# Hybrid gMLP and band-attention step: head pairs handled two to a cycle, with whole-row turning runs, streams beside the pairs and y gated in place

## The chip, the cores and the metric

One core of a Trainium2 chip runs the whole program in one launch. The metric is the device time of that launch in microseconds (us); the median of three runs stands for a kernel. Engines are named as in the profile: PE is TensorE, PEld its weight load, DVE VectorE, ACT ScalarE, POOL GpSimd, SP SyncE (here a DMA queue only).

## What is computed

2048 prompt tokens and 8 streams of 16 tokens (17 tiles of 128 tokens, width 1024) go through one layer:

```python
h = einsum(x, w_in)                       # u, v_a, z_a, q, k, v_b, z_b
u, v_a = gelu(h_u), layernorm(gelu(h_va))
a_out = u * (tril(w_s) @ v_a + b_s)       # chunks of 128, 4 groups
p = softmax(q @ k.T / 8 + rel_bias)       # chunk of 64 queries, its own and 8 chunks before, 8 heads
b_out = p @ v_b
y = concat(a_out * silu(z_a), b_out * silu(z_b))
out = layernorm(2**0.25 * x + y @ w_out)
```

The streams do the same with 128 cached keys and 16 new ones. The arithmetic is fp32, and each big product is made of three products of operands that are split into a high and a low part (high by high, high by low, low by high).

## The kernel before, in words

**Projections.** All groups of `w_in` are multiplied first, by `project_chunk` and `project_tile`. The last group, v, goes tile by tile (24 products of 128x512 a tile): the first `V_EARLY` = 9 tiles by themselves, and the other 8 inside the next stage, in halves.

**The paired stage.** A list `UNITS` holds 72 units: for each prompt tile t four "pair" units (two heads each), and after each of the tiles 4 to 11 one "stream" unit. One step of every engine's loop handles one unit, and PE's step is: `scores` of unit s (12 products from tile 4 on, 64 rows by 128 columns, two heads side by side, L1256), `turn(s-1, 0)` (up to 8 blocks of the probabilities transposed, in 16 half transposes, L1290), a `quarter` of dense work (12 products of 128x512: half a v tile up to step 15, L1186, then half of a half of the output projection, L1351), `turn(s-1, 1)` (the fifth key tile: 2 blocks, 4 half transposes, from tile 4 on), and `weigh(s-1)` (the weighted sums, up to 20 products, 128 rows by 64 columns, L1328). The output projection of tile n starts at step 16 + 4n (`START`).

**Around it.** DVE adds the bias and takes the row minimum (`add_bias`, L1050), then `normalise` multiplies by one over the row sum (L1067, L1069). ACT takes the exponent with its sum (L878) and copies the transposes out of PSUM (`copy_turned`, L871, two copies a unit from tile 4 on). After the fourth pair of a tile DVE's `gate` (L1076) multiplies the sums by z into a staging tile, SP stores it to `s_y` (L610), and `load_y` (L550) later brings the whole y tile back. ACT rounds it (`y_high_part`, L895), and DVE subtracts (L1139). After a half of the output projection DVE adds the residual (L1098) and takes statistics (L1101, L1109). POOL makes 1/sqrt(var) (L731, L733) and, for all but the last `TAIL` = 3 tiles, three passes over 128x1024: subtract and scale (L737), times gain (L740), plus offset (L742). For the last tiles DVE does it (`finish`). POOL also splits the output weights in eight parts j (`split_wo`, L716 and L718): parts 0 to 3 are loaded when v tile 13 is projected, and parts 4 to 7 when v tile 16 is. The first half of the output projection needs parts 0 to 3, the second parts 4 to 7.

**Order.** Every queue is written out by hand. All waits are on counting semaphores, and each engine runs its own list in order. SP issues nearly all DMAs and waits in its own list. The order of the tiles is 0 to 14, the streams' tile, then 15 (`ORDER`).

Of the kernel before, what the change touches and what calls it, by code (L numbers as in the profile page):

```python
# [33 lines left out]
TAIL = 3  # L34
# [23 lines left out]
V_EARLY = 9  # L58
# [70 lines left out]
STREAM_AFTER = 4  # L129

# [6 lines left out]
def unit_order():  # L137
    units = []
    for t in range(PTILES):
        units += [("pair", t, p) for p in range(GRP)]  # L140
        if STREAM_AFTER <= t < STREAM_AFTER + SB:
            units.append(("stream", t - STREAM_AFTER, None))
    return units


UNITS = unit_order()
NU = len(UNITS)
PLACE = {(kind, a, b): u for u, (kind, a, b) in enumerate(UNITS)}


def heads_of(u):
    return 2 if UNITS[u][0] == "pair" else 1


def turned_copies(u):

    kind, t, _ = UNITS[u]
    return 1 + (key_tiles(t) > 4) if kind == "pair" else 2
# [9 lines left out]
HEADS_BEFORE = before(heads_of)  # L168
COPIES_BEFORE = before(turned_copies)
STREAMS_BEFORE = before(lambda u: UNITS[u][0] == "stream")  # L170
TILES_BEFORE = before(lambda u: UNITS[u][0] == "pair" and UNITS[u][2] == GRP - 1)


def gate_step(tile):

    return PLACE["pair", tile, GRP - 1] + 2

V_STEPS = 2 * (TILES - V_EARLY)  # L180
STEPS = V_STEPS + 4 * TILES
ORDER = [*range(PTILES - 1), PTILES, PTILES - 1]
START = [V_STEPS + 4 * n for n in range(TILES)]
SPLIT = [s - 1 for s in START]
GATED = [gate_step(t) for t in range(PTILES)] + [PLACE["stream", SB - 1, None] + 3]
Y_LOAD = [max(START[max(n - 2, 0)] + 1 - 7 * (n < 2), GATED[ORDER[n]] + 1) for n in range(TILES)]
X_LOAD = [V_STEPS, V_STEPS] + [START[n - 2] + 7 for n in range(2, TILES)]
POOL_TILES = TILES - TAIL

# [27 lines left out]
def hybrid_stream_step(nc, x, x_t, w_all, w_o, w_sgu, b_sgu, ln_v_g, ln_v_b, rel_rev, ln_g, ln_b,  # L217
# [6 lines left out]
    with ctx:  # L224
# [11 lines left out]
        s_y = dram("s_y", [2 * GRP, P, T])  # L236
# [48 lines left out]
        prob = [at(f"prob{s}", x_at[1] + 12800 + 2560 * s, [WIN]) for s in range(4)]  # L285
        z = [at(f"z{s}", x_at[1] + 23040 + 2048 * s, [GRP, P]) for s in range(2)]
        pt = [at("pt0", x_at[1] + 27136, [10, P]), at("pt1", u_at, [10, P])]
        low, den, rden = (at(name, x_at[1] + 32256 + 64 * j, [4]) for j, name in enumerate(("low", "den", "rden")))
# [112 lines left out]
        so_kept = sem("so_kept")  # L401
        so_back = sem("so_back")
        ys_ready = sem("ys_ready")
        ys_stored = sem("ys_stored")

# [13 lines left out]
        def slot(unit, h):  # L421
            return (HEADS_BEFORE[unit] + h) % 4
# [1006 lines left out]
```

## Time and profile before

| | |
|---|---|
| median of 3 runs | 1085.3 us (1085.28 to 1085.33) |
| the profiled execution, its own time | 1085.31 us |
| its span in the profile | 1083.3 us |
| busy share of PE / DVE / ACT / POOL | 99% / 43% / 31% / 20% |
| the paired stage | 634 us to 1044 us of the span |

A time in a row is counted in us from the start of the span. A matmul's end is modelled, since matmuls overlap in the array, so the spacing of two starts tells more than the length of one. In the timeline a row is a run of like instructions, with the start of the first and the time to the end of the last. In the chain of waits a row is a piece of the work that ended last.

### The profile page before, as it was taken

To read this page: it belongs to the slowest core of one execution; us is meant where nothing else is said; L and a number is where in the kernel's file an instruction comes from. 1 tells how busy PE (TensorE), PEld (TensorE's weight loads), DVE (VectorE), ACT (ScalarE), POOL (GpSimd) and SP (SyncE) were. 2 spreads that over 40 slices of the span, in tenths; PEclk is the share of its full clock that TensorE was granted. 3 is DMA by queue.
4 is the path that set the end of the run, shared out by engine and by line. 5 is a ranking of instruction groups with operands and counts; after the bars stand their busy time and mean duration, and the time that the engine had idled before them with its cause. 6 is when DMAs were issued, how large, how long until landed. Compare 5 with 4: busy or idle time off the path is not lost.

```text
span 1083.3 us, 17667 instructions
## 1 busy us (share of the span) xinstructions
PE 1068.4 (99%) x7338; PEld 912.4 (84%) x7338; DVE 462.7 (43%) x940; ACT 333.6 (31%) x660; POOL 213.7 (20%) x163
## 2 busy tenths in 40 slices
PE   9999999999999999999999999999999999999997
PEld 7988889999999999999999877777777777788875
DVE  6544441212212111121112014577667767777755
ACT  6410101111111111111112134454554555555530
POOL 0111112010110000000000000553444333444331
PEclk9999999999999999999999999999999999999999
DMA  9561114221211333333331444795555445444422
GB/s 340 194 182 49 39 39 129 73 88 60 73 63 54 117 123 123 117 124 112 119 107 65 126 147 145 214 283 162 156 149 167 124 150 149 129 143 141 127 89 78
DMA packets 129967, 137.34 MB, mean 127 GB/s; under 512 B 7496, under 2 KB 103904, under 8 KB 129888
## 3 DMA queue, kind: packets, MB, share of 16 engines
q1 hardware_dynamic: 124992, 121.54, 35.5%
q10 hardware_dynamic: 4896, 14.68, 4.1%
q8 instruction: 58, 0.95, 0.4%
q14 instruction: 21, 0.17, 0.1%
HBM read 86.62 MB, written 52.72 MB: 129 GB/s over the span
## 4 chain that ended last, share of the span: by engine, by line
PE 93%; DVE 2%; POOL 2%; ACT 1%; DMA 1%; issue 1%; POOLq 0%; DVEq 0%; SPq 0%
PE s_ps L1169 35%; PE s_ps L1186 16%; PE out_ps L1351 14%; PE pt_ps L1169 8%; PE o_ps L1328 6%; PE s_ps L1256 5%; PE pt_ps L1290 4%; PE s_ps L1351 2%; DVE prob L1069 1%; POOL wo_l L718 1%; PE o_ps L1198 1%; PE out_ps L1198 1%; ACT prob L878 1%; DMA bias<-s_skew 1%; DMA wo_raw<-w_o 0%
## 5 line engine op out<-in xcount | busy, mean ns | idle before, releaser
L1169 PE MATMUL s_ps<-xh,ring 128*128 128x512 f32 (+1 forms) x1200 | 341.3, 362 | 0.8 <-ACT st L842 0.8
L1169 PEld LDWEIGHTS s_ps<-xh,ring 128*128 128x128 f32 x1200 | 221.3, 188 | 24.5 <-issue 1.2
L1169 PE MATMUL s_ps<-xl,ring 128*128 128x512 f32 (+1 forms) x600 | 217.2, 362 | 0.0
L1186 PE MATMUL s_ps<-ring,xh 128*128 128x512 f32 x544 | 171.0, 395 | 0.0
L871 ACT ACTIVATE pt<-pt_ps 128x1024 f32<-128x1024 f32 (+3 forms) x112 | 78.9, 704 | 158.6 <-PE pt_ps L1290 158.3
L1169 PEld LDWEIGHTS s_ps<-xl,ring 128*128 128x128 f32 x600 | 112.6, 188 | 11.8
L1186 PEld LDWEIGHTS s_ps<-ring,xh 128*128 128x128 f32 x544 | 99.8, 188 | 20.3
L1186 PE MATMUL s_ps<-ring,xl 128*128 128x512 f32 x272 | 106.1, 390 | 0.0
L1050 DVE CUSTOM_DVE_ANT_1 prob<-s_ps,bias 128x640 f32<-128x640 f32 (+1 forms) x112 | 85.5, 801 | 45.3 <-PE s_ps L1256 45.3
L1351 PE MATMUL out_ps<-wo_h,yh 128*128 128x512 f32 x248 | 103.0, 415 | 0.5 <-POOL wo_l L718 0.5
L878 ACT ACTIVATE prob<-prob,low 128x640 f32<-128x640 f32 (+3 forms) x136 | 100.3, 740 | 5.8 <-DVE low L1050 5.4
L1351 PE MATMUL out_ps<-wo_h,yl 128*128 128x512 f32 x248 | 97.0, 391 | 0.0
L1351 PE MATMUL out_ps<-wo_l,yh 128*128 128x512 f32 x248 | 96.8, 391 | 0.0
L1069 DVE TENSOR_SCALAR prob<-prob,rden 128x640 f32<-128x640 f32 (+4 forms) x136 | 94.6, 695 | 4.8
L1169 PE MATMUL pt_ps<-xh,ring 128*128 128x384 f32 x304 | 80.2, 334 | 0.0
L1328 PE MATMUL o_ps<-pt,v 128*64 128x128 f32 x1120 | 75.3, 278 | 0.0
L963 DVE SCALAR_TENSOR_TENSOR st<-s_ps,st 128x512 fp32r<-128x512 f32 (+1 forms) x32 | 20.0, 624 | 119.0 <-ACT st L803 119.0
L1256 PE MATMUL s_ps<-k,q 64*128 64x256 f32 (+3 forms) x696 | 70.4, 331 | 0.1
L1328 PEld LDWEIGHTS o_ps<-pt,v 128*64 128x64 f32 x1120 | 59.9, 137 | 8.9 <-issue 5.6
L1290 PEld LDWEIGHTS pt_ps<-ident,prob 64*128 64x128 f32 x1120 | 46.1, 138 | 24.7 <-issue 14.0
L952 DVE SCALAR_TENSOR_TENSOR st<-st,s_ps 128x512 f32<-128x512 f32 (+1 forms) x32 | 19.5, 618 | 109.8 <-ACT st L789 109.8
L1256 PEld LDWEIGHTS s_ps<-k,q 64*128 64x128 f32 x696 | 52.2, 185 | 13.4 <-issue 11.3
(138 smaller groups left out, 1237.4 us busy)
## 6 DMA issues: line engine op xcount, KB each, us to landing
raw<-w_all ACTq DMA_DIRECT2D x26, 512.0 KB, 3.6
yr<-s_y SPq DMA_DIRECT2D x17, 512.0 KB, 4.8
r<-x SPq DMA_DIRECT2D x17, 512.0 KB, 3.6
q<-s_q SPq DMA_DIRECT2D x16, 512.0 KB, 4.2
k<-s_k SPq DMA_DIRECT2D x16, 512.0 KB, 5.6
y_out<-r SPq DMA_DIRECT2D x15, 512.0 KB, 3.9
s_y<-st SPq DMA_DIRECT2D x24, 256.0 KB, 2.4
x_raw<-x_t SPq DMA_DIRECT2D x12, 384.0 KB, 12.9
```

Source lines behind the costliest of these rows:

```text
L871: nc.scalar.activation(held, pt_both[:, :, 0:m, :], ACT.Copy).then_inc(pt_copied, 1)
L878: nc.scalar.activation(prob[s][:, 0:n], prob[s][:, 0:n], ACT.Exp, bias=low[:, s:s + 1], scale=-1.0, accum_out=den[:, s:s + 1]).then_inc(ex ...
L963: nc.vector.scalar_tensor_tensor(out=st[s_low][:, 0:n].bitcast(f32r), in0=src, scalar=QSCALE if kind == "q" else 1.0, in1=held, op0=ALU.mu ...
L1050: nc.vector.tensor_tensor_reduce(out=out, in0=src, in1=b, scale=1.0, scalar=MASKED, op0=ALU.add, op1=ALU.min, accum_out=low[:, s:s + 1]).t ...
L1069: nc.vector.tensor_scalar(prob[s][:, lo:n], prob[s][:, lo:n], rden[:, s:s + 1], None, ALU.mult).then_inc(normed, 1)
L1169: last = nc.tensor.matmul(bank[b][:, 0:width], w[:, kc, :], xx[:, kc, :], start=kc == 0 and a == 0, stop=kc == KC - 1 and a == 2)
L1186: last = nc.tensor.matmul(out, xx[:, kc, cols], ring[:, 0:GRP, side, kc, :], start=kc == 0 and a == 0, stop=kc == KC - 1 and a == 2)
L1198: last = nc.tensor.matmul(mix_ps[t % 2][:, g * P:(g + 1) * P], st[t % 2][:, g * P:(g + 1) * P], (wt if t < PTILES else wts)[:, g, :], star ...
L1256: last = nc.tensor.matmul(s_ps[h][:, at_c:at_c + count * P], q[t % 2][rows, a * GRP + p, :], k[rows, c * GRP + p, first * P:(first + count ...
L1290: last = nc.tensor.transpose(pt_both[:, half, i, :], prob[slot(unit, h)][rows, lo + b * P:lo + (b + 1) * P], ident[rows, rows])
L1328: last = nc.tensor.matmul(o_ps[64 * h:64 * h + 64, p * P:(p + 1) * P], v[(t + 1 - nk + b) % KR][:, p * P + 64 * h:p * P + 64 * h + 64], pt ...
L1351: last = nc.tensor.matmul(out_bank(half), y[n % 2][:, c, :], w[h][:, c, :], start=c == 0 and a == 0, stop=c == KC - 1 and a == 2)
```

## The change

- The unit list holds the 64 pair units alone. One **cycle** handles two of them, 2c and 2c+1, in 38 cycles. `V_EARLY` is 13, so that four v tiles are left for cycles 0 to 3. The output projection of tile n is in cycles 4+2n and 5+2n, half of its columns each, 24 products in one run.
- PE's cycle is: turn of unit 2c-2, scores of 2c, the dense run (`middle`), a stream's part, turn of 2c-1, scores of 2c+1, and the sums of 2c-2 and 2c-1 one after the other.
- `turn` transposes all ten blocks in one run. The fifth key tile's two blocks go first, into columns 640 to 767 of the two score banks (`fifth_ps`), and so `turn` waits until both heads of the unit after next in the score order have been biased, and `scores` waits for the fifth tile's copies before its run at column 512. ACT copies the fifth tile in two copies and the rest in one.
- Stream b's scores are in cycle 7+2b, its transposes one cycle later, its sums two cycles later, with buffers and semaphores of their own.
- The y tile's attention half is gated straight into the y buffer (`yr`), so that its store to `s_y` is gone and the load is half as large. `yr` and `yl` share their memory. The streams' tile is last.
- The normalisation's first pass moves from POOL (L737) to ACT (`centre`, an Identity with scale and bias, two cycles after `START`), and POOL makes the bias for it (`shift`). `TAIL` is 4.
- DVE's cycle is: gate, bias of 2c, normalise 2c-1, the stream's normalise, normalise 2c, y's low part, residual, stream bias, stream gate, bias of 2c+1, statistics.

```diff
-V_EARLY = 9
+V_EARLY = 13
-TAIL = 3
+TAIL = 4
+UNITS = [(t, p) for t in range(PTILES) for p in range(GRP)]
+V_CYCLES = TILES - V_EARLY
+CYCLES = V_CYCLES + 2 * TILES
+START = [V_CYCLES + 2 * n for n in range(TILES)]
+STORE = [START[n] + (3 if n < TILES - TAIL else 2) for n in range(TILES)]
+STREAM_IN = [V_CYCLES + 3 + 2 * b for b in range(SB)]
...
+        z = [at(f"z{s}", x_at[2] + 16384 + 2048 * s, [GRP, P]) for s in range(2)]
+        yr = [at(f"yr{s}", x_at[3 + s] + 20480, [KC, P]) for s in range(2)]
+        fifth_ps = [s_ps[half][:, 640:768] for half in range(2)]
...
# SyncE
+                if cycle == 1:
                     sp.wait_ge(proj_done, DONE["v", 13])
                     for j in range(4):
                         load_wo(j)
...
+                if cycle == V_CYCLES - 1:
                     sp.wait_ge(proj_done, DONE["v", TILES - 1])
                     for j in range(4, 8):
                         load_wo(j)
                         if j % 2:
                             load_x(j // 2 - 2)
+                    store_v(V_EARLY + cycle)
...
# GpSimd
-                    nc.gpsimd.tensor_scalar(r[n % 2][:], r[n % 2][:], mv[n % 2][:, 0:1], rstd[n % 2][:],
-                                            ALU.subtract, ALU.mult).then_inc(centred, 1)
+                    nc.gpsimd.tensor_scalar(shift[n % 2][:], mv[n % 2][:, 0:1], rstd[n % 2][:], -1.0,
+                                            ALU.mult, ALU.mult).then_inc(shifted, 1)
                     pool.wait_ge(centred, n + 1)
...
# ScalarE
+            def copy_turned(unit):
...
+                if n > 4:
+                    act.wait_ge(turned, TURNED_BEFORE[unit] + 2)
+                    for half in range(2):
+                        held = pt[unit % 2][:, 8:10, HD * half:HD * half + HD]
+                        nc.scalar.activation(held, fifth_ps[half].rearrange("p (g t) -> p g t", g=2), ACT.Copy).then_inc(pt_copied, 1)
+                act.wait_ge(turned, TURNED_BEFORE[unit + 1])
...
+            def centre(n):
+                act.wait_ge(shifted, n + 1)
+                nc.scalar.activation(r[n % 2][:], r[n % 2][:], ACT.Identity, bias=shift[n % 2][:],
+                                     scale=rstd[n % 2][:]).then_inc(centred, 1)
+
+            for cycle in range(CYCLES):
+                copy_turned(2 * cycle - 2)
+                for h in range(2):
+                    exponent(2 * cycle, h)
+                if 1 <= cycle < V_CYCLES:
+                    copy_v(V_EARLY + cycle - 1)
...
+                    if START[n] - 1 == cycle:
+                        y_high_part(n)
...
+                    if START[n] + 2 == cycle:
+                        centre(n)
+                for b in at_cycle(cycle, -1):
+                    place_stream(b)
+                for b in at_cycle(cycle, 2):
+                    keep_sums(b)
+                for b in at_cycle(cycle, 1):
+                    copy_stream(b)
+                copy_turned(2 * cycle - 1)
+                for b in at_cycle(cycle, 0):
+                    stream_exponent(b)
+                for h in range(2):
+                    exponent(2 * cycle + 1, h)
...
# VectorE
+            for cycle in range(CYCLES):
+                if closes_tile(2 * cycle - 3):
+                    gate(UNITS[2 * cycle - 3][0])
+                biases(2 * cycle)
+                for h in range(2):
+                    normalise(2 * cycle - 1, h)
+                for b in at_cycle(cycle, 1):
+                    normalise_stream(b)
+                for h in range(2):
+                    normalise(2 * cycle, h)
...
+                        y_low_part(n)
...
+                    residual(n, h)
+                for b in at_cycle(cycle, 0):
+                    add_stream_bias(b)
+                for b in at_cycle(cycle, 2):
+                    gate_stream(b)
+                biases(2 * cycle + 1)
+                if n >= 0:
+                    statistics(n, h)
...
# TensorE
+            def turn(unit):
...
+                pe.wait_ge(normed, 2 * unit + 2)
+                if has_fifth(unit):
+                    pe.wait_ge(biased, min(2 * (unit + 2), 2 * NU))
...
+            for cycle in range(CYCLES):
+                turn(2 * cycle - 2)
+                scores(2 * cycle)
+                middle(cycle)
+                for b in at_cycle(cycle, 0):
+                    stream_scores(b, cycle)
+                for b in at_cycle(cycle, 2):
+                    weigh_stream(b, cycle)
+                for b in at_cycle(cycle, 1):
+                    turn_stream(b, cycle)
+                turn(2 * cycle - 1)
+                for b in at_cycle(cycle, 2):
+                    turn_back(b)
+                scores(2 * cycle + 1)
+                weigh(2 * cycle - 2)
+                weigh(2 * cycle - 1)
+                if cycle < V_CYCLES - 1:
+                    project_tile("v", V_EARLY + cycle, KC // 2, KC)
```

## Rows read from the trace of the kernel before

**Rows 1.** The page, busy time by engine.
```profile
PE 1068.4 (99%) x7338; PEld 912.4 (84%) x7338; DVE 462.7 (43%) x940; ACT 333.6 (31%) x660; POOL 213.7 (20%) x163
```
**Rows 2.** Busy time by stretch: span, length, each engine's busy, clock, DMA.
```profile
634.00:1044.20 410.20, 406.99 (x4026) 320.38 (x4024) 274.54 (x660) 211.76 (x458) 153.80 (x86) 1.00 0.52 155
...
996.96:1002.99 6.03, 6.03 (x67) 4.92 (x64) 4.95 (x9) 3.03 (x6) 4.58 (x2) 1.00 0.53 149
```
**Rows 3.** Timeline of PE, one unit: start, length, line, tiles, count.
```profile
1002.99 0.66 PE L1290 MATMUL pt_ps<-ident,prob 64*128 64x64 f32 x16
1003.58 0.50 PE L1351 MATMUL out_ps<-wo_h,yh 128*128 128x512 f32 x1
...
1006.52 0.34 PE L1290 MATMUL pt_ps<-ident,prob 64*128 64x64 f32 x4
1006.79 1.31 PE L1328 MATMUL o_ps<-pt,v 128*64 128x128 f32 x20
1008.03 1.15 PE L1256 MATMUL s_ps<-k,q 64*128 64x256 f32 x12
1009.02 0.66 PE L1290 MATMUL pt_ps<-ident,prob 64*128 64x64 f32 x16
```
**Rows 4.** The chain of waits, one half of the output projection alone.
```profile
1053.86 5.44 PE out_ps L1351 x24
```
**Rows 5.** Timeline of PE, a unit of tile 0: the short runs.
```profile
650.44 0.28 PE L1290 MATMUL pt_ps<-ident,prob 64*128 64x64 f32 x4
650.65 0.73 PE L1186 MATMUL s_ps<-ring,xh 128*128 128x512 f32 x2
...
653.59 0.44 PE L1328 MATMUL o_ps<-pt,v 128*64 128x128 f32 x4
653.96 0.39 PE L1256 MATMUL s_ps<-k,q 64*128 64x256 f32 x2
```
**Rows 6.** Timeline of PE, two waits, with the idle time before the row in brackets.
```profile
638.48 0.34 PE L1290 MATMUL pt_ps<-ident,prob 64*128 64x64 f32 x4 [0.68 <-DVE prob L1069]
...
1048.11 0.50 PE L1351 MATMUL s_ps<-wo_h,yh 128*128 128x512 f32 x1 [0.85 <-DVE r L1098]
```
**Rows 7.** The chain of waits, output weights 4 to 7: load, last split.
```profile
709.31 4.79 DMA wo_raw<-w_o
...
726.34 2.50 POOL wo_l L718
```
**Rows 8.** Groups by form, ACT from 634 us: busy, mean ns; idle before.
```profile
L895 ACT ACTIVATE yh<-yr 128x1024 fp32r<-128x1024 f32 x17 | 17.9, 1051 | 9.5 <-PE s_ps L1351 9.4
...
L901 ACT ACTIVATE so<-o_ps 128x128 f32<-128x128 f32 x8 | 2.2, 278 | 7.2 <-PE o_ps L1316 7.2
```
**Rows 9.** Timeline of ACT, the two exponents of a unit.
```profile
904.34 0.82 ACT L878 ACTIVATE prob<-prob,low 128x640 f32<-128x640 f32 x1
...
905.15 0.82 ACT L878 ACTIVATE prob<-prob,low 128x640 f32<-128x640 f32 x1
```
**Rows 10.** Timeline of DVE, the two biases of a unit.
```profile
1028.03 0.81 DVE L1050 CUSTOM_DVE_ANT_1 prob<-s_ps,bias 128x640 f32<-128x640 f32 x1
...
1028.76 0.82 DVE L1050 CUSTOM_DVE_ANT_1 prob<-s_ps,bias 128x640 f32<-128x640 f32 x1
```
**Rows 11.** Timeline of DVE: normalise beside a POOL pass, without one, of a stream.
```profile
742.17 2.65 DVE L1069 TENSOR_SCALAR prob<-prob,rden 128x640 f32<-128x640 f32 x1
...
744.92 0.55 DVE L1069 TENSOR_SCALAR prob<-prob,rden 128x640 f32<-128x640 f32 x1
745.39 0.68 DVE L1098 SCALAR_TENSOR_TENSOR r<-r,out_ps 128x512 f32<-128x512 f32 x1
...
765.74 0.30 DVE L1069 TENSOR_SCALAR prob<-prob,rden 128x144 f32<-128x144 f32 x1
```
**Rows 12.** Timeline of POOL, the pass of that time.
```profile
742.08 2.38 POOL L742 TENSOR_TENSOR r<-r,offset 128x1024 f32<-128x1024 f32 x1
```
**Rows 13.** Busy time by stretch, after PE's last product at 1075.6 us.
```profile
1076.00:1079.00 3.00, 0.00 (x0) 0.00 (x0) 2.53 (x4) 0.00 (x0) 1.36 (x2) 1.00 0.00 0
1079.00:1081.00 2.00, 0.00 (x0) 0.00 (x0) 1.41 (x2) 0.00 (x0) 0.28 (x1) 0.72 0.00 0
```

More of the change, by code:

```diff
@@ L124 @@
 ZA_COUNT = counted(("za",))
-STREAM_AFTER = 4
 def key_tiles(t):
     return min(t, 4) + 1
[L137 to L146, printed above, removed]
+UNITS = [(t, p) for t in range(PTILES) for p in range(GRP)]
 NU = len(UNITS)
-PLACE = {(kind, a, b): u for u, (kind, a, b) in enumerate(UNITS)}
-def heads_of(u):
-    return 2 if UNITS[u][0] == "pair" else 1
 def turned_copies(u):
-    kind, t, _ = UNITS[u]
-    return 1 + (key_tiles(t) > 4) if kind == "pair" else 2
+    return 3 if key_tiles(UNITS[u][0]) > 4 else 1
 def before(count):
@@ L165, in before, with at_cycle @@
     return out
-HEADS_BEFORE = before(heads_of)
 COPIES_BEFORE = before(turned_copies)
[L170 to L187, printed above, removed]
+TURNED_BEFORE = before(lambda u: 4 if key_tiles(UNITS[u][0]) > 4 else 2)
+V_CYCLES = TILES - V_EARLY
+CYCLES = V_CYCLES + 2 * TILES
+START = [V_CYCLES + 2 * n for n in range(TILES)]
+STORE = [START[n] + (3 if n < TILES - TAIL else 2) for n in range(TILES)]
+X_LOAD = [V_CYCLES, V_CYCLES] + [STORE[n - 2] for n in range(2, TILES)]
 POOL_TILES = TILES - TAIL
+SLOTS = 4
+STREAM_IN = [V_CYCLES + 3 + 2 * b for b in range(SB)]
+def at_cycle(cycle, later):
+    return [b for b in range(SB) if STREAM_IN[b] + later == cycle]
 def key_runs(t):
@@ L1278, in turn @@
                 else:
-                    pe.wait_ge(pt_copied, COPIES_BEFORE[unit] + e)
-                if kind == "stream":
-                    past, new = (pt_both[:, half].rearrange("p g t -> p (g t)")[:, 0:P] for half in range(2))
-                    nc.tensor.transpose(past, prob[slot(unit, 0)][:, 0:PAST], ident[:]).then_inc(turned, 2)
-                    nc.tensor.transpose(new[0:SN], prob[slot(unit, 0)][:, PAST:SKEYS], ident[:]).then_inc(turned, 2)
-                    return
-                lo, blocks = P if t == 2 else 0, min(8, 2 * key_tiles(t) - 8 * e)
+                    pe.wait_ge(pt_copied, COPIES_BEFORE[unit])
+                lo, blocks = P if t == 2 else 0, min(8, 2 * nk)
                 for i in range(blocks):
-                    b, h = (8 * e + i) // 2, i % 2
+                    b, h = i // 2, i % 2
                     for half in range(2):
```

413 lines of the change are left out of this document (215 added, 198 removed).

## The prediction

> **What bounds the kernel now.** I read the page's busy times first: PE is busy for 99% of the span, and no other engine for half of it [rows 1]. The busy times by stretch say the same of the paired stage, where all of the change lies: PE is busy for 407.0 of 410.2 us at the full clock, so 3.2 us of it are waits, and a unit takes 6.03 us [rows 2]. So the time is the sum of PE's runs, and the question is what it costs to break them. The timeline of PE shows that [rows 3]. From the start of a quarter of 12 products to the next run is 1006.52 - 1003.58 = 2.94 us. In the tail 24 such products in one run take 5.44 us, 0.227 each [rows 4], so 12 are worth 2.72, and a quarter pays 0.22 for coming in and going out. The four transposes of the fifth key tile take 0.27 (to 1006.79). A run of 16 takes 0.59 [rows 3] and a run of 4 behind scores 0.21 [rows 5], so four more in a run are worth 0.38 / 3 = 0.13. Twenty sums take 1.24 [rows 3] and four 0.37 [rows 5], so one is worth 0.054 and twenty more in a run 1.09.
>
> **What goes.**
> 1. Dense runs. The stage has 73 of them (steps 0 to 72). Afterwards there are 36: two in cycles 0 to 2, one in cycles 3 to 32. The v tiles 9 to 12 join the run ahead of the stage. 37 x 0.22 = 8.1 us.
> 2. The fifth key tile's own turning run, in 48 units: 48 x (0.27 - 0.13) = 6.9 us.
> 3. Two sums in one go, 32 times: 32 x (1.24 - 1.09) = 4.8 us.
> 4. The boundaries that the trace doesn't show: turn to scores, scores to dense, scores to sums, sums to turn. Behind scores, which have the same 64-row form, 16 transposes start at once (0.59), and behind dense work 4 cost 0.06 more than behind scores (0.27 against 0.21) [rows 3, 5]. At best turn to scores is as free as scores to turn, and the scores save an entry like the others' 0.2 per cycle, -6 us over 32 cycles. At worst each new boundary costs 0.05 more than the one that it replaces, +6. I take -2, nearer to the good end, since the forms are the same.
> Sum: -21.8 us. From tile 4 on a cycle is then 12.06 - 0.22 - 0.28 - 0.15 - 0.06 = 11.35 us.
> The Trainium skill, TensorEngine Tiling (Array Packing), Key Properties, states that a change of tiling mode drains TensorE and a change of tile within a mode doesn't. By it a pair of units goes from eight changes of form to four, and item 4 would be at its good end (-6). What the trace shows of scores to turn agrees; turn to scores no run here shows yet.
> 5. Waits: 3.2 us in the stage [rows 2], such as the 0.68 for the first normalise, and 0.85 for a bank behind it [rows 6], and about 1 more that the modelled ends hide. The turned units are now half a cycle or more older than their scores, so these go: -5 us.
>
> **What costs nothing.** The gate writes y in place: 16 stores and half of each y load go. They are on SP, and nobody on PE's path waits for them. The y load waits for the projection two tiles back and has over a cycle (11 us) until y is rounded. The gate itself now also waits for that projection, long done. Behind SP's wait for a finished tile and its store stand the next x, v and z loads, needed a cycle or more later; if POOL were a cycle late, the residual would wait for x. POOL's first pass becomes one ACT pass of about the 1.05 us of an equal one [rows 8], in an even cycle with no y to round; it has cover while ACT ends within the dense run of 5.4 us. The two edits of order (streams' tile last, TAIL 4) put 3 us more on DVE in cycle 31, behind which no scores are left.
>
> **What comes: new waits of PE.**
> a. Output weights. Parts 4 to 7 are loaded when v tile 16 is done; from the load's start to the last split are 1.4 us short of 21: 709.31 to 728.84 = 19.5 us [rows 7]. Before, PE had four steps until then. Now it has, after v 16, the turns (4 x 0.37), the scores (0.5 + 3 x 1.0), the sums of four units of tile 1 (2 x 1.03), the dense run of cycle 4 and the first half of cycle 5's (5.44 + 2.72, entries 0.2): 15.4 us. PE waits 19.6 - 15.4 = 4.2 us, once; with 0.2 around it 4.4. Bounds: 2 (cycles slowed by POOL's passes eat it) to 6.
> b. The fifth tile's copies. Frame: scores of 2c+1 end at 0. Biases start at 0.25, 0.73 apart, and end at 1.8 [rows 10]. The exponents are 0.81 apart [rows 9] and end at 2.8, and ACT's two copies of 128 columns (0.28 each, as the nearest row [rows 8]) at 3.45. PE sums for 2.33, turns for 0.65, and its scores reach column 512 at 3.2 to 3.7, by how the six k slots lie. So it waits 0.1 in most, 0.3 in a third: 24 cycles, 3 us (0 to 6).
> c. Stream copies ahead of scores in eight cycles (0.1), the small units of tiles 0 and 1 whose copies have little cover, early normalises beside POOL's splits: 2 us (0 to 5).
> d. POOL's passes and normalise. A normalise takes 0.55 us, and 2.65 where it starts inside POOL's offset pass: it ends with it [rows 11, 12]. Now the two passes start right behind ACT's `centre`, in even cycles. From the first bias: exponents at 0.87 and 1.68, centre at 2.5 to 3.6, POOL's gain pass at 3.75, offset pass to about 8.7. DVE: two biases to 1.6, two normalises of 2c-1 to 3.2 (0.8 each with the reciprocal), in a cycle with a stream its reciprocal and 0.30 [rows 11], and then the first normalise of 2c at 4.0. That is 0.2 too late: it waits to 6.4, the second starts at 6.8 inside the offset pass and waits to 9.0, the residual (0.68) ends at 9.7, and the biases of 2c+1 at 11.3. PE wants them before the fifth block's turn of 2c at 9.75. It waits 1.5 us, and then mostly 0.2 for item b's copies: 1.7. Eight even cycles (8 to 22) turn a stream: 13.6 us. In the other even cycles the first normalise starts at 3.4, before POOL, only the second waits (to 6.5), and the biases at 7.5 are in time.
>
> **Sum of the likeliest case.** -21.8 - 5 + 4.4 + 3 + 2 + 13.6 = -3.8 us. The profiled execution took 1085.31 us, 2 of it around its span of 1083.3, and the median is 1085.3, so both are one base: 1081.5, and I say 1081. PE's end to the last store (7.7 us) is unchanged.
>
> **Rivals.**
> - *POOL starts too late to catch the first normalise* (28%). The margin of item d is 0.2 us, in a chain of five steps whose ACT pass has scale and bias operands that no row shows. If it is 0.2 longer, only second normalises wait, which nobody notices: 1081.5 - 13.6 = 1068. For: 0.2 is thin. Against: it needs to be so in all eight cycles, and every step's length in the rows repeats to 0.05.
> - *DVE becomes the bound in every tile* (12%), the one that ends slower. Place: even cycles without a stream too. Price: the same 1.7 in 13 even cycles instead of eight, 8.5 more, and normalises late by a pass in the odd ones where y's low part stands (0.3 x 13): 1081.5 + 12.4 = 1094; with item 4 at its good end 1090. It decides once DVE is 0.4 us later, or POOL earlier, than I count in these cycles. Against: DVE is busy for 67% of the stage [rows 2], and has about 10 us of work in an odd cycle of 11.35 (four biases at 0.75, four normalises at 0.8, and the gate, y's low part, residual and statistics).
> - *The clock falls during wait a* (8%). After PE's last product the granted clock is full for over 3 us and then falls, to a mean of 0.72 in the next stretch, 0.5 being 1.2 GHz [rows 13]. Waits up to 0.85 us before it left the clock alone [rows 6]. If 4.4 us are enough and PE then runs at half speed for some 5 us, it loses 2.5 to 3: 1084. The Trainium skill, TensorE: Matmul & The Clock Gate, The HAM clock gate, says that an idle array is throttled to half rate by default. By that rule this case would be the likeliest; the trace agrees in kind (the fall at the end), and a wait of this length inside the work no run shows.
> - *The regrouping saves less than counted* (10%, both ways): boundaries at the bad end, 1089, or several small misses of the terms, 1075. That the runs aren't joined can't be: PE runs its list in order.
> - The case itself: 42%.
>
> **How the numbers follow.** From the trace, differences under 0.2% (2.2 us) are about what a measurement of this kernel can't tell from no change. The likeliest case has 1081 with its terms' bounds giving 1076 to 1087, so 72% of it is faster, 18% the same, 10% slower. Faster: 0.42 x 0.72 + 0.27 of the first rival's 0.28 + 0.03 of the clock's + 0.05 of the last = 0.65. Slower: 0.04 + 0.11 + 0.03 + 0.04 = 0.22. The same: 0.13. The range needs to hold the first rival, 1068 less 2, and goes up to 1088: it leaves out most of the slower rival and the far ends, about 2 in 10. The likeliest case's own range is 1076 to 1087.
>
> **What would show it.** In the trace after: dense runs of 24 at 5.44 to 5.7 us from start to next run; no transposes x4 by themselves; 40 sums in one run in 2.33. One PE wait of about 4 us for the split weights, some 45 us into the paired stage. In PE's waits the turn (or scores) held by DVE's bias of the unit after, eight times about 1.5 us, with normalises of over 2 us beside POOL's gain and offset passes. Right about items 1 to 3 and wrong about d: 1068. I am wrong altogether if PE waits in most cycles, if scores behind a turn start over 0.15 us late, or if PE's busy share is still 99% with a time near 1085.

## The result and the profile after

| | before | after |
|---|---|---|
| median | 1085.3 us | 1073.0 us (1072.6 to 1074.0, 4 runs) |
| profiled execution, its span | 1085.3, 1083.3 | 1074.0, 1071.9 |
| PE's last product ends | 1075.6 | 1064.3 |

The ratio of after to before is 0.9885 (95% interval 0.9873 to 0.9897): 12.4 us faster. The forecast was 1081, with a range of 1066 to 1088. So the sign and the range hold, but the sum is 8 us off, and its terms are further off than that: two of them cancel. I went through the same views as before. First the page's busy times, then the busy times by stretch (columns as in [rows 2]).

```profile
PE 1053.1 (98%) x7338; PEld 912.6 (85%) x7338; DVE 459.8 (43%) x944; ACT 353.0 (33%) x722; POOL 157.2 (15%) x160
```
```profile
655.15:1029.62 374.47, 371.19 (x3945) 303.95 (x3944) 274.27 (x665) 228.18 (x514) 106.33 (x84) 1.00 0.47 145
686.00:710.00 24.00, 22.06 (x194) 17.46 (x193) 20.47 (x41) 10.40 (x24) 13.70 (x8) 0.93 0.88 285
1050.00:1060.00 10.00, 8.95 (x30) 7.22 (x31) 6.21 (x10) 0.00 (x0) 1.65 (x2) 0.73 0.14 52
760.00:1000.00 240.00, 240.00 (x2736) 199.84 (x2735) 177.93 (x425) 156.11 (x348) 59.43 (x50) 1.00 0.43 130
```

PE has lost 15.3 us of busy time with the same 7338 matmuls, as against [rows 1]. The last row is the one to look at: over 240 us, with seven of the eight cycles that turn a stream, PE is busy for all of it. The prediction had put its largest wait there. The idle time and the low clock (0.93 and 0.73 in rows two and three) lie before and behind that stretch. The timeline of PE shows one cycle without a stream, the answer to [rows 3].

```profile
946.65 0.34 PE L1352 MATMUL s_ps<-ident,prob 64*128 64x64 f32 x4
946.83 0.67 PE L1365 MATMUL pt_ps<-ident,prob 64*128 64x64 f32 x16
947.30 1.23 PE L1323 MATMUL s_ps<-k,q 64*128 64x512 f32 x12
948.46 2.40 PE L1394 MATMUL o_ps<-pt,v 128*64 128x128 f32 x40
950.80 0.34 PE L1352 MATMUL s_ps<-ident,prob 64*128 64x64 f32 x4
...
952.51 0.50 PE L1430 MATMUL out_ps<-wo_h,yh 128*128 128x512 f32 x1
...
957.90 0.39 PE L1430 MATMUL out_ps<-wo_h,yl 128*128 128x512 f32 x1
958.22 0.34 PE L1352 MATMUL s_ps<-ident,prob 64*128 64x64 f32 x4
```

From turn to turn this is 958.22 - 946.65 = 11.57 us (12.06 before, 11.35 forecast). Twenty transposes take 0.65, forty sums 2.34, twenty-four dense products 5.71.

The waits of PE in the paired stage and after it, in the view of waits (total, times, longest):

```profile
PE out_ps L1430 <- DVE yl L1180: 4.8, 1, 4.8
PE pt_ps L1365 <- DVE prob L1102: 1.9, 2, 1.2
PE s_ps L1323 <- DVE low L1078: 1.2, 1, 1.2
```

**The early loss.** Timeline of PE:

```profile
697.25 0.59 PE L1365 MATMUL pt_ps<-ident,prob 64*128 64x64 f32 x12 [0.72 <-DVE prob L1102]
699.07 1.13 PE L1323 MATMUL s_ps<-k,q 64*128 64x128 f32 x12 [1.23 <-DVE low L1078]
...
700.49 0.63 PE L1430 MATMUL out_ps<-wo_l,yh 128*128 128x512 f32 x1
700.91 0.63 PE L1430 MATMUL out_ps<-wo_h,yl 128*128 128x512 f32 x1
...
703.87 0.40 PE L1430 MATMUL out_ps<-wo_h,yh 128*128 128x512 f32 x1
```

and of POOL and of DVE at that time:

```profile
694.62 2.36 POOL L711 TENSOR_TENSOR wo_l<-wo_raw,wo_h 128x1024 fp32r<-128x1024 f32 x1
```
```profile
694.86 2.34 DVE L1102 TENSOR_SCALAR prob<-prob,rden 128x384 f32<-128x384 f32 x1
```

A normalise of 384 columns takes 2.34 us (0.42 with POOL idle), because it ends only 0.21 behind POOL's subtraction of the output weights: the hold of [rows 11, 12] in a place that the prediction hardly looked at. PE waits 1.3 (until 674.7 us), 0.8 and 1.4 us, with two small ones 4.0 in all. These are the rows' brackets and up to 0.2 more, which the modelled ends hide. Then products come 0.43 apart instead of 0.227, until 703.87: half clock, 1.6 us more.

**The tail loss.** The chain of waits at the end (start, length, what):

```profile
1039.15 1.43 DVE r L1165 x2
1040.60 3.58 DMA y_out<-r
...
1044.19 0.33 SPq L549
...
1044.57 3.92 DMA yr<-s_y
...
1051.05 7.79 PE out_ps L1430 x24
1058.83 5.45 PE s_ps L1430 x24
```

The last tile's y load stands on SP behind the store of tile 14 and behind the x load that waits for this store. So it starts at 1044.57, PE waits 4.8 us for y's low part, and the run that follows takes 7.79 instead of 5.45. That is 7.2 us that no step of the prediction had.

In the middle of the stage the order is another one (SP's queue, a tile with `STORE` three cycles after its `START`):

```profile
839.91 0.36 SPq L600 DMA_DIRECT2D y_out<-r  x1
842.59 0.34 SPq L549 DMA_DIRECT2D r<-x  x1
...
854.38 0.42 SPq L544 DMA_DIRECT2D yr<-s_y  x1
```

There too SP waits for the tile before it stores: POOL's offset pass ends at 839.88. But the y load comes 14 us later, and ACT rounds this y at 870.30. The last `TAIL` tiles are stored two cycles after their `START`, which puts the store into the same cycle as the y load, directly ahead of it.

### The profile page after: what moved, and what is told of

The parts are those of the page before. It is cut to its first block, busy times and chain, and to the rows that moved or that the text cites. A ratio compares the mean times of both kernels' runs of the same rounds, so it can differ in the third digit from the quotient of the medians.

```text
span 1071.9 us, 17673 instructions
## 1 busy us (share of the span) xinstructions
PE 1053.1 (98%) x7338; PEld 912.6 (85%) x7338; DVE 459.8 (43%) x944; ACT 353.0 (33%) x722; POOL 157.2 (15%) x160
## 4 chain that ended last, share of the span: by engine, by line
PE 97%; DVE 1%; DMA 1%; issue 0%; POOL 0%; POOLq 0%; ACT 0%; DVEq 0%; ACTq 0%; SPq 0%
PE s_ps L1228 35%; PE s_ps L1245 17%; PE out_ps L1430 16%; PE pt_ps L1228 8%; PE o_ps L1394 6%; PE s_ps L1323 6%; PE pt_ps L1365 3%; PE s_ps L1352 1%; PE s_ps L1430 1%; PE o_ps L1257 1%; PE out_ps L1257 1%; PE o_ps L1408 0%; PE out_ps L1264 0%; PE s_ps L1272 0%; DMA yr<-s_y 0%
## 5 line engine op out<-in xcount | busy, mean ns | idle before, releaser
L873 ACT ACTIVATE prob<-prob,low 128x640 f32<-128x640 f32 (+3 forms) x128 | 97.6, 764 | 57.5 <-DVE low L1078 57.5
L865 ACT ACTIVATE pt<-pt_ps 128x1024 f32<-128x1024 f32 (+3 forms) x64 | 60.5, 945 | 27.9 <-PE pt_ps L1365 25.6
L1394 PE MATMUL o_ps<-pt,v 128*64 128x128 f32 x1120 | 68.3, 276 | 0.0
L1430 PEld LDWEIGHTS out_ps<-wo_h,yh 128*128 128x128 f32 x248 | 47.5, 191 | 20.1 <-DVE yl L1180 5.2
L1245 PEld LDWEIGHTS s_ps<-ring,xl 128*128 128x128 f32 x272 | 51.1, 188 | 10.8
```

What stands on the lines that cost most here:

```text
L865: nc.scalar.activation(held, pt_both[:, :, 0:m, :], ACT.Copy).then_inc(pt_copied, 1)
L873: nc.scalar.activation(prob[s][:, 0:n], prob[s][:, 0:n], ACT.Exp, bias=low[:, s:s + 1], scale=-1.0, accum_out=den[:, s:s + 1]).then_inc(ex ...
L1245: last = nc.tensor.matmul(out, xx[:, kc, cols], ring[:, 0:GRP, side, kc, :], start=kc == 0 and a == 0, stop=kc == KC - 1 and a == 2)
L1394: last = nc.tensor.matmul(o_ps[64 * h:64 * h + 64, p * P:(p + 1) * P], v[(t + 1 - nk + b) % KR][:, p * P + 64 * h:p * P + 64 * h + 64], pt ...
L1430: last = nc.tensor.matmul(out_bank(half), y[n % 2][:, c, :], w[h][:, c, :], start=c == 0 and a == 0, stop=c == KC - 1 and a == 2)
```

## The experiments

All edits are made in the changed kernel, except where two are joined. Intervals are those of the ratio to the kernel before.

**1. The y loads of the last two tiles ahead of the store.**

```diff
                     for j in range(4):
                         load_wo(j)
+                for n in range(TILES - 2, TILES):
+                    if START[n] - 2 == cycle:
+                        load_y(n)
                 for n in range(TILES):
                     if STORE[n] == cycle and n < TILES - 2:
...
                 for n in range(TILES):
-                    if START[n] - 2 == cycle:
+                    if START[n] - 2 == cycle and n < TILES - 2:
```


> The changed kernel, with SyncE issuing the y loads of the last two tiles ahead of the store and the x load of the same cycle. My theory (the tail wait): in the changed kernel the store of tile 14 waits for VectorE's last pass until 1040.6 us, the x load behind it for the store to land at 1044.2, and only then the last y load starts, which makes TensorE wait 4.8 us and run 2.3 us longer at half clock. So with the load first: no wait of TensorE for y's low part, full clock to the end, time 1073.0 - 7.2 = 1065.8 us (1064.5 to 1067). Rival (the wait only hides another one, since the streams' gate, the rounding and the split of the last tile are late too): TensorE still waits over 2 us in the same place, 1070 to 1073.

Measured: 1066.4 us, 0.9823 (0.9807 to 0.984), 6.6 less than the change. SP's queue:

```profile
1035.30 0.37 SPq L544 DMA_DIRECT2D yr<-s_y  x1
1040.49 0.34 SPq L603 DMA_DIRECT2D y_out<-r  x1
1044.06 0.33 SPq L549 DMA_DIRECT2D r<-x  x1
```

The load now starts 9 us earlier, the wait for y's low part is not among PE's waits, and the granted clock from 1050 to 1060 us is 1.00. The tail loss is shown: it was the order of SP's queue.

**2. The subtraction that splits the output weights as a plain copy.** It leaves the low part of the output weights wrong (their whole value stands there).

```diff
-                nc.gpsimd.tensor_tensor(wo_l[h][held], wo_raw[h][held], wo_h[h][held].bitcast(f32),
-                                        ALU.subtract).then_inc(wo_done, 1)
+                nc.gpsimd.tensor_copy(wo_l[h][held], wo_raw[h][held]).then_inc(wo_done, 1)
```


> The changed kernel, with GpSimd's subtraction of the high part of the output weights replaced by a plain copy, so that the low part of the weights is wrong. It takes one input where the subtraction takes two. My theory: the waits of TensorE at 670, 695 and 697 us (1.3, 0.8 and 1.2 us) come from normalises that stand inside GpSimd's two-input passes (2.1 to 2.5 us each instead of 0.3 to 0.4), and their sum of 3.3 us is what makes the clock fall (1.6 us more in the dense run at 700 us). With one input the normalises take about 1 us at most: under 1 us of waits, clock full between 686 and 710 us, 1073.0 - 4 = 1069 us (1068 to 1070.5). Rival A (any big pass of GpSimd holds a normalise): waits stay over 2.5 us, 1072 to 1073. Rival B (VectorE's order makes them late, not GpSimd): the same 1073.

Measured: 1069.1 us, 0.985 (0.9835 to 0.9864). In the stretch from 686 to 710 us PE is busy for 23.7 of 24 us at a clock of 1.00. So POOL's subtraction was behind the waits and the slow clock. But it isn't its two inputs alone that hold a normalise, as the run was meant to show: the copies hold it too (timelines of POOL and of DVE).

```profile
690.43 1.04 POOL L709 CAST wo_h<-wo_raw 128x1024 fp32r<-128x1024 f32 x1
```
```profile
690.62 1.07 DVE L1101 TENSOR_SCALAR prob<-prob,rden 128x384 f32<-128x384 f32 x1
```

All seven normalises that begin inside a copy end 0.08 to 0.21 behind it and take 0.74 to 1.07 us instead of 0.29 to 0.42. A copy lasts 1.04 us and a subtraction 2.4; that shorter hold was enough to leave PE one wait of 0.3.

**3. The split moved to ACT (high part) and DVE (low part).**

```diff
-            for j in range(4):
-                split_wo(j)
...
-            for j in range(4, 8):
-                split_wo(j)
...
# ScalarE
+                for j in {2: (0, 1), 3: (2, 3), 4: (4, 5)}.get(cycle, ()):
+                    wo_high_part(j)
...
# VectorE
+                for j in {2: (0, 1), 3: (2, 3), 4: (4, 5)}.get(cycle, ()):
+                    wo_low_part(j)
...
+                if cycle == 4:
+                    wo_low_part(6)
+                    wo_low_part(7)
```


> The changed kernel, with the whole split of the output weights taken from GpSimd: ScalarE makes the high parts and VectorE the low ones, parts 0 and 1 in cycle 2, parts 2 and 3 in cycle 3, parts 4 to 7 in cycle 4. My theory: no normalise is held before 715 us, so the waits of 3.3 us and the clock's loss of 1.6 us go, and VectorE's eight passes of 1.2 us fit beside the dense runs: 1073.0 - 4.5 = 1068.5 us (1067 to 1070.5). Rival: VectorE's own passes take the place, TensorE waits for the biases or for part 7 in cycles 4 and 5 by 2 us or more: 1071 to 1074.

Measured: 1069.6 us, 0.9854 (0.984 to 0.9869); of PE's waits before 715 us one of 0.4 is left (at 675 us), and from 686 to 710 us PE is busy for 24.0 of the 24 us. So 3.3 us came back, a little less than expected, and the tail loss stayed.

**4. Both, 1 and 3.**

> The changed kernel with the y loads of the last two tiles first and the split of the output weights moved from GpSimd to ScalarE and VectorE. The two losses lie 330 us apart, so they should add: 1073.0 - 7.2 - 4.5 = 1061.3 us (1059.5 to 1063.5), the granted clock full from the first products to the last. Rival (one loss comes back elsewhere): over 1065.

Measured: 1062.6 us, 0.9798 (0.9777 to 0.9819), the sum of the two gains (6.6 + 3.3) within 0.5. One of its four executions took 1067.2, the others 1062.0 to 1062.7. It is 22.9 us faster than the kernel before and 10.4 us faster than the change.

**5. The dense run in two halves of 12 again**, the second behind the turn of 2c-1.

```diff
                 project_out(n, h, 0, 4)
-                project_out(n, h, 4, 8)
...
                     turn_back(b)
+                if cycle >= V_CYCLES:
+                    project_out(*divmod(cycle - V_CYCLES, 2), 4, 8)
                 scores(2 * cycle + 1)
```


> The changed kernel, with the dense run of 24 products of a cycle cut in two runs of 12: the first where it was, the second behind the turn of 2c-1 and ahead of the scores of 2c+1. It undoes the joining of the quarters. Theory 1 (a cut costs what a run pays for coming in and going out, 0.22 us): 28 cuts, 1073.0 + 6.2 = 1079 us. Theory 2 (what costs is each change of the tile form, and turn to scores lost one too, so the cut adds two changes, with 0.12 more behind the turn and 0.1 more at the scores' first products): 28 x 0.45, 1073.0 + 12.5 = 1085.5 us. The trace should show which: the gap from the last transpose to the next product, now 0.03 us, at 0.15, and the scores' run longer by 0.1.

Measured: 1099.9 us, 1.013 (1.0115 to 1.0145), worse than either theory. From the last start of a turn to a dense run are 0.154 us, where turn to scores are 0.033, and the two halves take 2 x 2.94 against 5.65: with both, 0.35 a cycle, 10 us in 28 cycles. That part bears out the second theory in kind, that a change of form is what costs; its price of 0.45 was high. The other 17 us are waits that neither theory had. The residual now starts after the second half, the stream's bias (L1089) stands behind it on DVE, and the scores wait for that:

```profile
PE s_ps L1323 <- DVE low L1089: 8.8, 8, 1.1
...
PE s_ps L1373 <- DVE prob_s L1109: 4.3, 8, 0.6
```

**6. The sums of each unit apart.**

```diff
                     turn_back(b)
+                weigh(2 * cycle - 2)
                 scores(2 * cycle + 1)
-                weigh(2 * cycle - 2)
                 weigh(2 * cycle - 1)
```


> The changed kernel, with the sums of unit 2c-2 ahead of the scores of 2c+1, between turn and scores, and those of 2c-1 behind them, as two runs of 20. Theory 1 (only the joining of the two runs of sums counts, 0.15 us): 31 x 0.15, 1073.0 + 4.7 = 1077.5 us. Theory 2 (each change of tile form costs 0.15 to 0.2, and this adds two a cycle): 31 x 0.35, 1073.0 + 11 = 1084 us. Rival: the scores come later, so that biases and exponents come later by 1.3 us against the fifth block's turn, whose cover shrinks from 2.3 us to 1.2 (biases take 1.8): another 0.6 us a cycle from tile 4 on, 1073.0 + 11 + 14 = 1098 us.

Measured: 1106.1 us, 1.0186 (1.0169 to 1.0203). Three parts: form changes, about 0.29 in each of 31 cycles, 9 us; the fifth tile's turn comes 0.85 behind the sums instead of 0.20, in 24 cycles, 15 us (the biases of 2c+1 have lost half their cover, as the rival said, and at about its price: 0.64 a cycle for 0.6); and the stream's turned sums hold the next sums by 0.75, eight times, 6 us. Most of the joined sums' worth is cover, not the 0.15 for which the prediction counted them:

```profile
PE s_ps L1352 <- issue: 13.2, 23, 0.6
PE o_ps L1394 <- issue: 5.5, 8, 0.7
```

**7. The centring pass ahead of the exponents on ACT.**

```diff
                 copy_turned(2 * cycle - 2)
+                for n in range(POOL_TILES):
+                    if START[n] + 2 == cycle:
+                        centre(n)
                 for h in range(2):
                     exponent(2 * cycle, h)
...
-                for n in range(POOL_TILES):
-                    if START[n] + 2 == cycle:
-                        centre(n)
```


> The changed kernel, with ScalarE's centring pass ahead of the exponents of unit 2c instead of behind them. GpSimd's gain pass then starts 2.5 us earlier in its cycle, about 1.4 us after the first bias, and its offset pass 2.5 us after that. This tests the price of item d of the prediction, which did not come true because the first normalise of 2c escaped by 0.4 us. My theory: the first normalise of 2c-1 stands inside the gain pass and the second inside the offset pass, the biases of 2c+1 are late by 1 to 1.5 us in the eight cycles with a stream's turn and by 0.5 to 1 in the other even ones, and the turn of 2c-1 waits 1 us for its normalise: 13 cycles x 1 to 1.5, 1073.0 + 16 = 1089 us (1083 to 1093). Rival (normalises are late but nobody notices, there is slack): 1073 to 1075.

Measured: 1095.6 us, 1.0092 (1.0075 to 1.0109). The gain and offset passes now start 1.1 and 3.6 us after the first bias and hold both normalises of 2c-1 (timeline of DVE), so the stream's, behind them, is late, and PE's transposes of the stream wait for it eight times:

```profile
869.46 2.15 DVE L1102 TENSOR_SCALAR prob<-prob,rden 128x640 f32<-128x640 f32 x1
871.71 2.48 DVE L1102 TENSOR_SCALAR prob<-prob,rden 128x640 f32<-128x640 f32 x1
```
```profile
874.65 0.33 PE L1373 MATMUL s_ps<-ident,prob_s 128*128 128x128 f32 x1 [1.36 <-DVE prob_s L1109]
```

The expectation had the two held normalises, but put the loss in the stream's cycles at the biases of 2c+1. Those came in time: PE's eight waits for the stream are 1.5 to 1.7 us each with what the modelled ends hide, 12.9 together, and four more, for the normalises of 2c-1 in cycles without a stream, are 4.4. After two of the eight (847 and 901 us) the granted clock was at half for a while, which cost 1.5 us each time. So the expectation was right in kind, by another waiter.

**8. The first pass of the normalisation on POOL again.**

```diff
-                    nc.gpsimd.tensor_scalar(shift[n % 2][:], mv[n % 2][:, 0:1], rstd[n % 2][:], -1.0,
-                                            ALU.mult, ALU.mult).then_inc(shifted, 1)
+                    nc.gpsimd.tensor_scalar(r[n % 2][:], r[n % 2][:], mv[n % 2][:, 0:1], rstd[n % 2][:],
+                                            ALU.subtract, ALU.mult).then_inc(centred, 1)
...
-                for n in range(POOL_TILES):
-                    if START[n] + 2 == cycle:
-                        centre(n)
```


> The changed kernel, with the first pass of the normalisation back on GpSimd (3.8 us), behind its 1/sqrt, and ScalarE's pass left out. It undoes that part of the change. My theory: the three passes start at the end of the odd cycle, the gain pass then starts within 0.5 us of where it is now, it still holds at most one normalise a tile, and the tile is finished before its store: 1073 us (1072 to 1075). Rival A (GpSimd's passes are late for the store, so that x and residual come late): over 1076. Rival B (the first normalise of 2c is caught, as in item d, 1.5 us in eight cycles): 1085.

Measured: 1095.7 us, 1.0092 (1.0077 to 1.0107). My theory fell. The timeline of DVE in a stream cycle whose first bias starts at 758.76, and of PE:

```profile
762.57 2.23 DVE L1106 TENSOR_SCALAR prob_s<-prob_s,rden 128x144 f32<-128x144 f32 x1
...
764.91 2.60 DVE L1099 TENSOR_SCALAR prob<-prob,rden 128x640 f32<-128x640 f32 x1
```
```profile
770.35 0.34 PE L1349 MATMUL s_ps<-ident,prob 64*128 64x64 f32 x4 [0.90 <-issue]
```

POOL's gain pass began at 762.21 and its offset pass at 764.78. The stream's normalise is held by the one, the first normalise of 2c by the other; the transposes of the stream wait 0.6 to 0.7 (in seven of the eight stream cycles, 4.7 us), and the fifth tile's turn waits 0.8 to 1.9 in every second cycle, 13.0 us in the eleven from 740 to 1020 us. So the part of the change that the prediction put down at nothing, the pass to ACT, is worth 22.7 us inside this order.

**9. Three tiles for TAIL again, in the best version.**

```diff
-TAIL = 4
+TAIL = 3
```


> The best version so far (y loads first, output weights split on ACT and DVE: 1062.6) with TAIL = 3 again: tile 13's last passes on ACT and POOL instead of DVE. Theory (the prediction put this edit at nothing, since no scores are left behind it): 1062.6, within 0.2%. Rival (with the last store of y and x in a row on SP, a later store of tile 13 holds up the loads, or DVE's 3 us more sat ahead of y's low part in the last cycles): 1060 to 1061, or 1065 and more if the store of tile 13 comes late.

Measured: 1062.5 us, 0.9785 (0.9771 to 0.98): no difference from run 4, as the prediction had it.

**10. Five spare reciprocals on DVE behind the stream's normalise.**

```diff
+EXTRA = 5
...
                 nc.vector.tensor_scalar(prob_s[:], prob_s[:], rden[:, SLOTS:SLOTS + 1], None, ALU.mult).then_inc(s_normed, 1)
+                for k in range(EXTRA):
+                    nc.vector.reciprocal(rden[:, SLOTS + 1 + k:SLOTS + 2 + k], den[:, SLOTS:SLOTS + 1])
```


> Five spare reciprocals of 128x1 (0.15 us each) stand on DVE behind the stream's normalise in the eight cycles that turn a stream. Nothing else is changed. In the changed kernel the first normalise of unit 2c started 3.42 us after the first bias of the cycle and POOL's gain pass 3.83 after it; now the normalise should start at about 4.1. Theory (item d of the prediction is right as a mechanism and was missed by a margin of 0.4 us): it is held to the end of the gain pass (length about 2.5), the second is held by the offset pass (2.5), the biases of 2c+1 end about 11.0 us after the first bias, PE wants them at 10.1 to 10.3, and so waits 0.8 to 1.1 in each of eight cycles: 1073 + 7.5 = 1080.5, range 1079 to 1083. By the prediction's own price (1.7 each) 1086.5. Rival (the hold is there but PE never waits for these biases, since the runs ahead have slack): 1073 to 1075.

Measured: 1073.4 us, 0.9887 (0.9871 to 0.9904), no difference from the change. It doesn't decide: the five took 0.32 us together, not 0.75, and the normalise still started 0.11 ahead of the gain pass.

**11. Eleven of them** (`EXTRA = 11`).

> As the run with five spare reciprocals, but with eleven. Five took 0.32 us together (0.065 each in a row), so that the first normalise of unit 2c started 3.72 after the cycle's first bias and still 0.11 before POOL's gain pass; eleven should move it to 4.1, behind the start of the pass. Theory (item d of the prediction): it is now held to the end of the gain pass at 6.4, the second is held by the offset pass to 9.1, the biases of 2c+1 end about 11.2 us after the first bias, PE wants them at 9.9 to 10.1, and waits about 1.1 in each of eight cycles: 1073 + 9 = 1082, range 1079 to 1087 (its upper end is the price of 1.7 in the prediction). Rival (the pass catches the normalise, but PE has slack for it, or a normalise that comes just behind the start of a pass isn't held): 1073 to 1075.

Measured: 1090.1 us (1087.0 to 1092.9), 1.005 (1.0031 to 1.0068). Its timelines of DVE, POOL and PE in a stream cycle:

```profile
759.40 0.82 DVE L1079 CUSTOM_DVE_ANT_1 prob<-s_ps,bias 128x640 f32<-128x640 f32 x1 [1.46 <-PE s_ps L1326]
...
763.48 2.48 DVE L1103 TENSOR_SCALAR prob<-prob,rden 128x640 f32<-128x640 f32 x1
...
766.06 2.48 DVE L1103 TENSOR_SCALAR prob<-prob,rden 128x640 f32<-128x640 f32 x1
...
769.05 0.81 DVE L1079 CUSTOM_DVE_ANT_1 prob<-s_ps,bias 128x640 f32<-128x640 f32 x1
```
```profile
763.22 2.38 POOL L733 TENSOR_TENSOR r<-r,gain 128x1024 f32<-128x1024 f32 x1 [4.02 <-ACT r L918]
765.68 2.50 POOL L735 TENSOR_TENSOR r<-r,offset 128x1024 f32<-128x1024 f32 x1
```
```profile
743.22 0.34 PE L1355 MATMUL s_ps<-ident,prob 64*128 64x64 f32 x4 [1.92 <-DVE low L1079]
...
770.72 0.34 PE L1355 MATMUL s_ps<-ident,prob 64*128 64x64 f32 x4 [1.40 <-issue]
```

This is item d of the prediction, as it was written: the first normalise starts 4.08 after the first bias and is held, the second is held, the biases of 2c+1 start 9.65 after it, and the fifth tile's turn comes 1.4 to 1.5 us late (1.7 forecast) in seven of the eight stream cycles, 10.2 us together. In the first of the eight it comes 2.0 us late, and the granted clock is at half behind that wait: the turn, the scores and the dense run that follow take 1.4 us more than in the other cycles. Against run 10, moving one instruction by 0.36 us in eight cycles costs 14 us in the profiled execution, of which these parts are 13.6, and 17 in the median. Why the four executions lie 6 us apart, I did not settle.

Not tried: the y tile's store and load as they were, the streams inside the pairs' list, and the fifth tile's blocks turned apart from the others. What these parts are worth by themselves stays open.

## Why the prediction was right and wrong

The sign and the range came true, and in part by luck. The largest term (d, 13.6 us) did not come, and two losses that the sum lacked or had too small, 5.6 us early and 7.2 in the tail, filled most of its place. With both taken away the kernel takes 1062.6 us (run 4), which is below the range.

PE's runs and waits in the paired stage and the tail, added up from its timeline, give the change in PE's end: -18.8 for the runs, -5.3 for old waits, +12.9 for new waits and low clock, -11.2 in all. Each part is good to about 0.5 us, since a matmul's end is modelled.

1. **Dense runs** (-8.1 forecast): 245.4 us before, and 236.5 after without the waits and the half clock, about -9. The term was right, a little small; a run of 24 takes 5.56 to 5.71.
2. **The fifth tile's own run and the unseen boundaries** (items 2 and 4, -8.9 together). Turns -10.4, scores +4.3, the streams' part +1.5: -4.6. Twenty transposes take the 0.65 that was forecast, and turn to scores are 0.033 apart, so this boundary is free. But what the turn saved in going out, the scores now pay: 0.205 from their last start to a dense run or to sums. And the streams' part, at a place of its own, has changes of form that the prediction left out. The Trainium skill, TensorEngine Tiling (Array Packing), Key Properties, puts the cost on a change of mode: runs 5 and 6 agree (0.154 from turn to dense or to sums, 0.033 from turn to scores). The end of the range that I had hung on that rule (-6) did not come, since fewer changes are not free changes.
3. **Sums joined** (-4.8): -4.8, the forecast to the tenth, and yet run 6 shows that apart they would cost 33 us more, by the cover that they give the biases.
4. **Old waits** (-5): -5.3.
5. **Wait a, the output weights** (+4.4): not there. The last split ended at 704.0, 18.6 us after the load's start (19.5 worked out). PE came to the second half of the run at 704.6, 19.1 us after it, where the prediction had 15.4: the waits of 0.8 and 1.4 and the 1.6 of half clock had held it up. That is the reason item a gave for its lower bound (cycles slowed by POOL's passes), and it went below it. In runs 7 and 8, where the same waits came but the clock stayed full, PE did wait for the last split, 0.9 us. Run 3, with the split finished early, has no such wait.
6. **Item b, the fifth tile's copies** (+3): 0 between 740 and 1029 us. The margin was taken too short.
7. **Item c** (+2) is the term that was mis-sized: the normalises beside POOL's splits cost 3.5 us, small waits 0.5, and the clock 1.6. The prediction had the hold of [rows 11] and applied it to the gain and offset passes only.
8. **Item d** (+13.6): the step that failed is "the first normalise of 2c at 4.0. That is 0.2 too late". In the changed kernel (DVE, POOL and ACT, a stream cycle with its first bias at 757.08):

```profile
760.50 0.55 DVE L1102 TENSOR_SCALAR prob<-prob,rden 128x640 f32<-128x640 f32 x1
...
761.16 2.48 DVE L1102 TENSOR_SCALAR prob<-prob,rden 128x640 f32<-128x640 f32 x1
```
```profile
760.91 2.38 POOL L732 TENSOR_TENSOR r<-r,gain 128x1024 f32<-128x1024 f32 x1 [4.01 <-ACT r L917]
```
```profile
759.59 1.23 ACT L917 ACTIVATE r<-r,shift,rstd_o 128x1024 f32<-128x1024 f32 x1
```

The normalise starts at 3.42 and not 4.0: two of them are 0.66 apart, not 0.8, which makes 0.3 for the two of 2c-1, and the biases and the stream's part were rounded up by 0.1 and 0.2. POOL starts at 3.83, as forecast (3.75). So it is ahead by 0.4, the second is held and nobody waits. The first rival ("POOL starts too late to catch the first normalise", 1068) is what happened in this place; its 1068 has neither the tail loss (7.2) nor the lower a and b. The chance of 28% for it was a judgement on a margin of 0.2 us with an error of 0.6 in it. Run 11 shows the price to have been about right (12.2 us of waits for 13.6), runs 7 and 8 that the same hold bites for other waiters when the passes start earlier or DVE is held before. Run 8 is the second rival, "DVE becomes the bound in every tile", with its place (even cycles without a stream too) and its price (0.8 to 1.9 each, 1095.7 for the 1094 forecast), at the point where POOL makes all three passes.

9. **What was costed at nothing.** "Behind SP's wait for a finished tile and its store stand the next x, v and z loads": the list leaves out the y load, and this is the second failed step, 7.2 us. In the middle of the stage SP does wait for each tile before it stores, but the y load comes 14 us behind that store. In the last cycles the store stands directly ahead of it, and it is the load that PE waits for. TAIL was worth nothing, as said (run 9, with the y loads first). ACT's pass took 1.23, not 1.05.
10. **The clock.** The rival had the fall during wait a. It fell twice elsewhere: behind waits of 0.8 and 1.4 us that end at 697 and 699 us (1.6 us lost) and behind the 4.8 us in the tail (2.3 lost), where the rival had put 2.5 to 3. With the waits gone (runs 3 and 1) the granted clock is 1.00 in both stretches. The Trainium skill, TensorE: Matmul & The Clock Gate, The HAM clock gate, has an idle array throttled; the trace agrees. But the early fall isn't certain with its waits: in runs 7 and 8 they came and the clock stayed full.

From forecast to result: d -13.6, a -4.4, b -3, c +2, clock +1.6, tail +7.2, regrouping +3.0, old waits -0.3. That is -7.5, and 1081.5 - 7.5 = 1074.0 is the profiled execution.

## What to carry to other kernels

Before you move a pass of POOL, or anything of DVE ahead of it, write down for each cycle when each normalise and each pass starts: here 0.4 us decide over 13 us, and the hold is worth looking for beside POOL's gain, offset and subtraction passes and its casts, in weight splits too. When an order is turned into cycles, go through SP's list for the last tiles by themselves: a store that waits for the slowest engine must not stand ahead of a load that the next run needs. And count a regrouping by the cover that it gives the other engines as well as by its changes of form; here the second was 0.3 us a cycle and the first 0.7 (run 6).

## What the runs showed of the hardware

- A normalise on DVE that starts inside POOL's gain, offset or split subtraction ends just behind that pass: 2.48 to 2.61 us for 0.55, in all eight stream cycles of the change. From the pass's end it is 0.35 us with 640 columns and 0.08 with 128. POOL's casts of the output weights hold it in the same way, but they last 1.04 us only (0.87 to 1.06 us in the five cases of the change, seven of seven in run 2). Beside POOL's subtract-and-scale pass (3.8 us) it isn't held, at 0.55 to 0.61 us in 22 of 24 cases of the kernel before; the other two are a stream's, 0.70 and 1.09 for 0.30. In run 8 the eleven that began in that pass's last 1.0 us took 1.20 to 1.36. The Trainium skill, SBUF — State Buffer, Who interferes with whom, has the first to come keep a shared pair of ports for its whole instruction and the other wait, where DVE's instruction is in a two-port mode; the two-input passes and the casts agree, the subtract-and-scale pass mostly doesn't.
- The granted clock fell to half after two short waits of PE close together, with work of half a microsecond between them: 0.7 and 1.2 us by the rows' brackets in the change, 0.2 to 0.5 and 1.2 in runs 1, 10 and 11. In runs 7 and 8 such waits (0.5 and 0.6, and 1.2) left it full. Of single waits, those of 4.5 to 5.2 us in the tail were followed by half clock in every run that had one; of those of 1.4 to 1.5 in runs 7 and 8 three of ten were; of those of 1.9 the one in run 11 was and the ones in runs 5 and 8 were not; those of 1.3 to 1.4 in run 11 (seven) and of up to 0.85 in the kernel before [rows 6] were not.
- From the start of a run's last product to the next run are 0.033 us where the form stays (turn to scores), 0.154 from turn to dense, 0.205 from scores to dense or sums, and 0.319 from dense to turn, of which 0.227 are the dense product's own time.
- Eleven reciprocals of 128x1 in a row took 0.76 us, 0.07 each, where one before a dependent instruction takes 0.15.
